# Numbering the slots of the split weights by weight chunks alone

## Time and profile before

| what | value |
|---|---|
| median of three runs | 2343.22 us |
| the profiled execution, its own time | 2340.59 us |
| its span in the profile | 2338.8 us |
| TensorE busy | 2282.1 us (98%) |
| VectorE busy | 1677.7 us (72%) |
| ScalarE busy | 1029.0 us (44%) |
| moved by DMA | 430 MB, mean 184 GB/s |

### The profile page before, as it was taken

How to read it: one execution, slowest core, us unless ns; L and a number is a source line. 1 busy time by engine, 2 the same in 40 slices (tenths; PEclk the granted TensorE clock), 3 DMA queues, 4 the chain that set the end, 5 groups by cost and what they waited for, 6 DMA issues and landing times.

```text
span 2338.8 us, 30869 instructions
## 1 busy us (share of the span) xinstructions
PE 2282.1 (98%) x11041; PEld 1888.1 (81%) x11041; DVE 1677.7 (72%) x2394; ACT 1029.0 (44%) x1474; POOL 75.9 (3%) x113
## 2 busy tenths in 40 slices
PE   8999999999999999999999999999999899999997
PEld 6878788877878878777778888888888798999876
DVE  5479876688788877686878675857865878666644
ACT  5565655555556555344352222213322634544432
POOL 1022200000000000000000000000000000000000
PEclk9999999999999999999999999999999999999999
DMA  7966645667677766787756464646654467422243
GB/s 240 217 179 201 186 146 170 187 220 226 214 224 222 225 216 212 232 261 235 253 184 187 146 193 143 195 144 197 225 181 149 121 185 218 129 76 63 73 154 133
DMA packets 225945, 430.33 MB, mean 184 GB/s; under 512 B 13847, under 2 KB 38671, under 8 KB 224688
## 3 DMA queue, kind: packets, MB, share of 16 engines
q1 hardware_dynamic: 222112, 418.96, 58.3%
q10 hardware_dynamic: 3152, 9.83, 1.3%
q0 software_dynamic: 576, 0.14, 0.0%
HBM read 426.16 MB, written 2.72 MB: 183 GB/s over the span
## 4 chain that ended last, share of the span: by engine, by line
PE 68%; issue 18%; DVE 6%; DMA 5%; ACT 3%; DVEq 0%; ACTq 0%; POOL 0%; SPq 0%; POOLq 0%
PE ps L616 40%; PE ps L651 13%; PE ps L628 9%; DMA raw<-in_w_down 3%; DVE ada_acc L585 2%; DVE lo L556 2%; ACT hi L552 1%; DMA raw<-in_w_up 1%; PE ps L2412 1%; PE ps L665 1%; PE ps L2308 1%; DVE ustage L1769 1%; ACT ustage L1342 0%; PE ps L2172 0%; PE ps L805 0%
## 5 line engine op out<-in xcount | busy, mean ns | idle before, releaser
L552 ACT ACTIVATE hi<-raw 128x1024 fp32r<-128x1024 f32 x604 | 634.4, 1060 | 1074.2 <-PE ps L616 536.7
L556 DVE TENSOR_TENSOR lo<-raw,hi 128x1024 fp32r<-128x1024 f32 x604 | 732.0, 1223 | 457.3 <-ACT hi L552 455.1
L585 DVE SCALAR_TENSOR_TENSOR ada_acc<-raw,csil,ada_acc 128x512 f32<-128x512 f32 x720 | 492.4, 748 | 3.5 <-DMA raw<-in_ada_w 3.5
L616 PE MATMUL ps<-hi,h_hi 128*128 128x512 f32 x960 | 382.1, 398 | 2.6 <-DVE lo L556 2.6
L616 PE MATMUL ps<-hi,h_lo 128*128 128x512 f32 x960 | 378.9, 395 | 0.0
L616 PE MATMUL ps<-lo,h_hi 128*128 128x512 f32 x960 | 378.8, 395 | 0.0
L616 PE MATMUL ps<-hi,g 128*128 128x512 f32 x704 | 227.9, 398 | 11.3 <-DVE lo L556 11.2
L616 PEld LDWEIGHTS ps<-hi,h_hi 128*128 128x128 f32 x960 | 180.8, 188 | 46.8 <-DVE lo L556 6.0
L616 PEld LDWEIGHTS ps<-hi,h_lo 128*128 128x128 f32 x960 | 180.8, 188 | 42.3
L616 PEld LDWEIGHTS ps<-lo,h_hi 128*128 128x128 f32 x960 | 180.8, 188 | 40.6
L616 PEld LDWEIGHTS ps<-hi,g 128*128 128x128 f32 x704 | 132.4, 188 | 48.0 <-DVE lo L556 17.6
(11 more groups left out here) (328 smaller groups left out, 3430.2 us busy)
## 6 DMA issues: line engine op xcount, KB each, us to landing
raw<-in_ada_w SPq DMA_DIRECT2D x192, 512.0 KB, 4.2
raw<-in_w_up SPq DMA_DIRECT2D x176, 512.0 KB, 4.5
raw<-in_w_down SPq DMA_DIRECT2D x88, 512.0 KB, 5.1
raw<-in_w_in SPq DMA_DIRECT2D x84, 512.0 KB, 4.6
raw<-in_pool_w_in SPq DMA_DIRECT2D x64, 512.0 KB, 4.2
raw<-in_mla_w_in SPq DMA_DIRECT2D x56, 448.0 KB, 3.9
raw<-in_w_out SPq DMA_DIRECT2D x32, 512.0 KB, 3.8
raw<-in_pool_w_out SPq DMA_DIRECT2D x32, 512.0 KB, 4.5
```

The costliest lines, as they stand in the source:

```text
L552: act.activation(hi[:, slot, :, :], raw[:, slot, :, :], ACT.Copy).then_inc(hi_split, 1 + ada)
L556: dve.tensor_tensor(lo[:, slot, :, :], raw[:, slot, :, :], hi[:, slot, :, :].bitcast(F32), ALU.subtract).then_inc(lo_split, 1)
L585: ins = dve.scalar_tensor_tensor(acc, raw[:, slot, k, :], csil[:, v, kt:kt + 1], acc, ALU.mult, ALU.add)
L616: mm = pe.matmul(ps[:, bank, 0:n], tokens(a, kt0 + k, tok), w[:, slot, k, col0:col0 + n], start=first and k == 0 and s == 0, stop=last and ...
```

## The change

`hi` and `lo` get a numbering of their own. The slot of a weight chunk there is the number of weight chunks before it, modulo 4 (`split_slot`). `raw` keeps `c % RING`. The split no longer waits until place `c - 4` of the stream is used, but until the weight chunk four weight chunks back is (`slot_before`). In the loops, whose body stands for several turns, the nearer of the distances of its first two turns is taken. TensorE and VectorE read and write the new slots.

```diff
+WEIGHTS_BEFORE = list(itertools.accumulate((int(not of_ada) for of_ada, _ in STREAM), initial=0))
+WEIGHT_AT = [c for c, (of_ada, _) in enumerate(STREAM) if not of_ada]
+def weights_before(c):
+    return WEIGHTS_BEFORE[min(c, len(STREAM))] + max(c - len(STREAM), 0)
+def split_slot(c):
+    return weights_before(c) % RING
+def slot_before(c):
+    w = weights_before(c) - RING
+    return (WEIGHT_AT[w] if w < len(WEIGHT_AT) else len(STREAM) + w - len(WEIGHT_AT)) if w >= 0 else c - RING
...
-        def split_hi(act, c, slot, turn, ada):
+        def split_hi(act, c, slot, turn, ada, to, back):
             act.wait_ge(raw_loaded[slot], 16 * (turn + 1))
-            act.wait_ge(chunks_used, c + 1)
-            act.activation(hi[:, slot, :, :], raw[:, slot, :, :], ACT.Copy).then_inc(hi_split, 1 + ada)
+            act.wait_ge(chunks_used, c + used(1) - back)
+            act.activation(hi[:, to, :, :], raw[:, slot, :, :], ACT.Copy).then_inc(hi_split, 1 + ada)
-        def split_lo(dve, c, slot):
+        def split_lo(dve, c, slot, to):
             dve.wait_ge(hi_split, c + 1)
-            dve.tensor_tensor(lo[:, slot, :, :], raw[:, slot, :, :], hi[:, slot, :, :].bitcast(F32),
+            dve.tensor_tensor(lo[:, to, :, :], raw[:, slot, :, :], hi[:, to, :, :].bitcast(F32),
                               ALU.subtract).then_inc(lo_split, 1)
...
                 if not is_ada(c):
-                    split_hi(act, i * step + c, c % RING, i * (step // RING) + c // RING, ada_behind(c))
+                    turns = [c + i * step] if isinstance(i, int) else [c, c + step]
+                    back = min(at - slot_before(at) for at in turns)
+                    split_hi(act, i * step + c, c % RING, i * (step // RING) + c // RING, ada_behind(c), split_slot(c), back)
...
-                by_tokens(pe, i * len(order) + at, at % RING, a_hi, a_lo, CK_T * j, outs, width, j == 0, j == n - 1, ada_behind(at))
+                by_tokens(pe, i * len(order) + at, split_slot(at), a_hi, a_lo, CK_T * j, outs, width, j == 0, j == n - 1, ada_behind(at))
```

More of the change, by code:

```diff
@@ L1 @@
+import itertools
 import math
@@ L157, in is_ada @@
     return c < len(STREAM) and STREAM[c][0]
+WEIGHTS_BEFORE = list(itertools.accumulate((int(not of_ada) for of_ada, _ in STREAM), initial=0))
[7 more added lines that the diff above has]
+    return (WEIGHT_AT[w] if w < len(WEIGHT_AT) else len(STREAM) + w - len(WEIGHT_AT)) if w >= 0 else c - RING
+assert weights_before(C_HEADS) % RING == 0 and len(UP_ORDER) % RING == len(DOWN_ORDER) % RING == 0
 def ada_behind(c):
@@ L599, in los @@
                 else:
-                    split_lo(dve, i * step + c, c % RING)
+                    split_lo(dve, i * step + c, c % RING, split_slot(c))
         def tokens(a, kt, tok):
@@ L638, in panel_by_tokens @@
                 at = first + place(order, j0 + j)
-                by_tokens(pe, i * len(order) + at, at % RING, a_hi, a_lo, CK_T * j, outs, width, j == 0, j == n - 1, ada_behind(at))
+                by_tokens(pe, i * len(order) + at, split_slot(at), a_hi, a_lo, CK_T * j, outs, width, j == 0, j == n - 1, ada_behind(at))
         def first_chunk(pe, c, first, last, kt0, width, half, a_hi, a_lo):
             at = first_at(c)
-            slot, nk = at % RING, CK_T * W // width
+            slot, nk = split_slot(at), CK_T * W // width
             pe.wait_ge(lo_split, at + RING + 1)
@@ L2364, in first_pool_panel @@
             def first_pool_panel():
-                part = lambda s, j, frees: by_tokens(pe, C_POOL + j, (C_POOL + j) % RING, h4_hi, h4_lo, CK_T * j, streams[s * TT:(s + 1) * TT],
+                part = lambda s, j, frees: by_tokens(pe, C_POOL + j, split_slot(C_POOL + j), h4_hi, h4_lo, CK_T * j, streams[s * TT:(s + 1) * TT],
                                                      W, j == 0, False, ada_behind(C_POOL + j), frees)
@@ L2383, in first_pool_panel @@
                     at = C_POOL + place(POOL_ORDER, j)
-                    by_tokens(pe, at, at % RING, h4_hi, h4_lo, CK_T * j, streams, W, False, j == CH - 1, ada_behind(at))
+                    by_tokens(pe, at, split_slot(at), h4_hi, h4_lo, CK_T * j, streams, W, False, j == CH - 1, ada_behind(at))
             def pool_group(i, e):
@@ L2397, in chunk @@
                     at = C_POOL + place(POOL_ORDER, e * POOL_W + CH + j)
-                    by_channels(pe, i * step + at, at % RING, *a, ada_behind(at))
+                    by_channels(pe, i * step + at, split_slot(at), *a, ada_behind(at))
                 pe.wait_ge(y_gated, FREE + n * 4)
@@ L2465, in part @@
                     at = start + place(order, CH + j)
-                    return by_tokens(pe, at, at % RING, y_hi, y_lo, CK_T * j, which, W, j == 0, j == CH - 1, ada_behind(at), frees)
+                    return by_tokens(pe, at, split_slot(at), y_hi, y_lo, CK_T * j, which, W, j == 0, j == CH - 1, ada_behind(at), frees)
                 if last:
```

## The result

| | before | after |
|---|---|---|
| median | 2343.06 us | 2320.87 us |
| runs | 2341.62 to 2344.21 | 2320.34 to 2324.18 |
| the profiled execution, its own time | 2340.59 us | 2320.34 us |
| its span | 2338.8 us | 2318.5 us |

The ratio is 0.9912, 95% interval 0.9899 to 0.9924: 22 us less. The prediction said 2328.1, and its range ended at 2323. The direction was right, the size too small.

A forecast was written before the change was run, and what follows sets the result against it. TensorE was taken as the bound, busy 2282.1 of 2338.8 us, its waits on splits 17.8 us. The stage and clock terms summed to 15.1 us, taking the median from 2343.2 to 2328.1 us, range 2323 to 2336.

The forecast's parts named there:

- FIRST: Wait of 2.51 us at 165 us stays; some split waits ahead of it go: 0.3 us (bounds 0, 1).
- behind a long series on ScalarE that doesn't change: Reason given in FIRST for keeping TensorE's wait of 2.51 us at 165 us, leaving only 0.3 us to win.
- UP: Five turns, each with a split waiting long for TensorE; all of TensorE's waits go: 5.7 us (bounds 2.6, 5.7).
- some 2 us more: Added to the upper bounds: the first matmul after a stall is a long one (0.50 us), at 16 places.
- DOWN, first turn: First stall of 2.62 us stays, a mid-turn wait for TensorE loosens: 1.3 us (bounds 0, 2.4).
- if the ring starts 1.33 us sooner, it ends sooner by as much: Step for DOWN's first turn, carrying VectorE's 1.33 us wait for a split through to the turn's end: 1.3 us.
- a load is late instead: Rival: looser splits find their chunk not landed, so only part is won; 8.6 us, 2334.6, or 2331 to 2332; chance 0.31.
- DOWN, second turn: Splits around the start come one weight chunk earlier, so TensorE's four waits go: 2.8 us (bounds 1.3, 2.8).
- POOL: At its end two splits waited for TensorE and VectorE reached the modulation sums too late: 0.8 us (bounds 0, 0.8).
- MLA: Stall of 3.53 us at 1964 us shrinks by 1.8 us; the clock behind it stays up, 2.4 us more.
- The signs: Expected in the profile after: TensorE's waits on splits fall from 17.8 to 6 or 7 us; over 10 in DOWN refutes.
- slower by longer loads: Rival: more loads in flight make each take longer, DOWN's ring having no slack; 2355 at 1.4 us a load; chance 0.03.

The follow-up runs named there:

- first_47: Changed kernel's slots, looser waits only for FIRST's splits behind a modulation chunk up to place 47, all others as before; single run 2338.89 us beside 2336.13 of before.
- up_five: Changed kernel with the waits of before everywhere except five splits of UP, one in each turn, that wait for the fourth weight chunk back; 2340.41 us, ratio 0.9997.
- keep_74: Changed kernel, but the 74 splits that waited for the second weight chunk back (5 in UP) keep their wait of before; 2329.1 us, ratio 0.9952.
- ctx_pieces: Changed kernel with the 2 MB context load issued in 8 pieces of 256 KB, one after every third split of DOWN's first turn; 2321.41 us.
- changed_again: The changed kernel unaltered, run again for its spread; 2321.21 us, ratio 0.9914 to before.
- down_only: Changed kernel with the looser waits in DOWN alone, the waits of before in all other stages; 2337.92 us, ratio 0.9988.

## Why the prediction was wrong in size

**FIRST** (0.3 predicted, 3.8 measured) is the largest miss. Between the average of the ten traces with looser waits in all or most of FIRST and that of the seven with none lie 4.0 us. The step that failed is "behind a long series on ScalarE that doesn't change". The series starts earlier if the splits ahead of it do, and first_47 shows that two waits carry 1.3 us. The stalls at 227 and 274 us were not in the prediction, since I went by the whole span's largest waits. The prediction also says that the clock did not fall after the stall of 2.51 us. That is right for its one trace, but in four others it fell, and this price is missing in its sum. Some 0.9 us of the 3.8 is no gain of the waits: at the very start a matmul follows the one before by 0.43 us up to 16.2 us in before, and by 0.23 us from 14.3 us on in the changed kernel. These are the distances at the two levels of the clock (the records of the granted clock begin only with the rise, at 17.07 and 14.04 us), and this start differs between executions of one kernel too.

**UP** (5.7, measured 6.7). The amount was nearly right, the reason half. The prediction let one split in each turn, with its wait of 4.45 us, stand for the gain. up_five shows that it alone gives nothing, keep_74 that without it some 5 of the 6.7 us are lost. The rest is the restart after each stall: in before the matmul at 859.79 us started 0.83 us after the one ahead of it (at 858.96 us), with 0.44 us of recorded idle time. In the changed kernel it is

```profile
849.07 0.40 PE L641 MATMUL ps<-hi,h_lo 128*128 128x512 f32 x1
849.30 0.47 PE L641 MATMUL ps<-hi,h_hi 128*128 128x512 f32 x1
```

0.23 us. So 0.60 us were won where 0.44 are shown as idle: 0.16 more. Ten stalls make 1.6 us in UP by that. The prediction had this as "some 2 us more" in its upper bound and left it out of its sum. Its working there sets the length of a matmul (0.50 us) against the distance of two starts (0.23 us), which are different things; beside the usual length of 0.39 us the first matmul is 0.11 us longer.

**DOWN, first turn** (1.3, measured 0.2; in the other kernels with looser waits in DOWN and full loads and sums -1.5 to -0.1, in those with the waits of before -1.4 to 1.7). The step "if the ring starts 1.33 us sooner, it ends sooner by as much" failed. The lower bound, "0, if the load is late instead", is what happens: the chain there goes from load to load (5.20 and 4.16 us in the lines above), and half loads win 9.5 us where the looser waits won nothing. ctx_pieces is 2.3 us sooner at 956 us and has lost all of it 98 us later. The rival "a load is late instead" was right for this turn alone.

**DOWN, second turn** (2.8, measured 3.5, and 2.3 and 3.1 in changed_again and down_only; 2.2 us between the averages of the two groups of kernels). Right, and for the reason given: the chain no longer leaves TensorE where it did. One stall of 1.3 us remained.

**POOL** (0.8, measured 1.0 with POOL_OUT). Right; 0.9 of it is the step at the end of POOL.

**MLA** (4.2, measured 2.9, and 4.6 in changed_again). The stall lost 2.4 us of idle time, where the sum had 1.8, and the lower clock behind it is gone, as predicted, which gives another 2.4 us. In the first profile another stretch at the lower clock, at 1816 us, took 1.6 us back. That this term may come and go, as the prediction also had it, was met with the waits of before alone (the clock stayed up in down_only).

**Heads and last product** (0, measured 2.0). No wait changed there. Before had two stretches at a lower clock, at 2224 and at 2234 us, the changed kernel one, at 2214. In the other traces it is none, one or two, so nothing shows this to be the change's. Together with the offset of the medians (2 us) it is the part of the miss that no reading of one trace gives, and that it went the same way as the rest is chance. The terms of FIRST and UP (4.5 us too small together) are the rest; those of DOWN and MLA were 0.4 and 1.3 us off the other way.

**The signs.** TensorE's waits on splits went to 11.0 us, not to "6 or 7". The prediction's own terms do not give 6 or 7 either: 17.8 less 2.6, 1.3, 2.8 and 1.8 is 9.3. The rest lies mainly in DOWN: its first turn kept 7.7 of its 8.4 us, and one stall of 1.3 us stayed in its second. Its waits in DOWN stayed under 10 us (9.0), and no stage that had none got one.

The rival "slower by longer loads" is refuted for this change: from 925 to 1000 us the median load of w_down took 5.0 us, and 5.1 before, as over the whole span. The Trainium skill (DMA: Bandwidth & Descriptors, Latency and other measured facts) says that memory answers in 0.2 us on average and in 2 us at high load; the runs here show no such step from before to after.

## What to carry to other kernels

A ring that several engines pass through seems to have one pace, set by its tightest step. Loosening one wait shows as nothing until the others are loose too (0 and 1.7 us alone, over 6 together), so ask of each looser wait what would be late next, and follow it back one round: a load that looks punctual may only be hidden by the wait. Short stalls cost more than their recorded idle time, so take them from the distance between the starts of two matmuls. And a row of work on another engine that doesn't change can still start earlier; look at what stands ahead of it before calling a stall fixed.

## What was not expected of the hardware

- Behind two stalls of the same length, 3.41 us, at the same matmul, the granted clock was 0.50 in one execution and 1.00 in another. Behind the stall of 2.5 us in FIRST it fell in four of seven traces, behind one of 1.2 us in none of eleven.
- A stall of TensorE cost 0.16 us beyond its recorded idle time (0.60 against 0.44 us).
- Halving a load from 512 to 256 KB in DOWN brought its median from 5.0 to 3.3 us, not to half.
- Single stretches at the lower clock come and go where no wait was changed: the heads and the last product had none, one or two of them.
